# HGRN: odd heads mirrored instead of odd chunks, and POOL's low part in four pieces

## The chip, the cores and the metric

One core of one Trainium2 chip runs the whole program in one launch. The metric is the device time in microseconds (us), median of the runs shown. The engines are TensorE (PE), VectorE (DVE), ScalarE (ACT), GpSimd (POOL) and SyncE (SP); each works through its own queue, and they are tied by semaphores only.

## The reference

Two transformer blocks at sequence length 512 and width 1024, all in float32. The first has an HGRN2 mixer (8 heads of 128), an MLP of 4096 with squared ReLU, latent attention and a second MLP; the second has sparse attention, a state-space mixer and a gated feed-forward layer of 2816 with short convolutions. The change touches the HGRN2 mixer and the preparation of weights:

```python
q = silu(xn @ w_q); forget = lb + (1 - lb) * sigmoid(xn @ w_f); k = 1 - forget; v = xn @ w_i
# per head and chunk, b = cumsum(log(forget)) along time:
scores = einsum('bhtd,bhsd,bhtsd->bhts', q, k, exp(b_t - b_s) for s <= t else 0)
o = scores @ v + (q * exp(b)) @ state
state = exp(b_last) * state + (k * exp(b_last - b)).T @ v
out = (rmsnorm(o, g_norm) * silu(xn @ w_g)) @ w_o
```

## The kernel before

**Weights.** All large weights come as one stream of 375 tiles of 128x1024 in four slots. A float32 product is made of three fp32r products: x_hi with w_hi, x_lo with w_hi, x_hi with w_lo. SP loads the raw tile (L397), POOL issues a cast DMA for w_hi (`cast`, L404) and subtracts, w_lo = w_raw - w_hi, in one operation of 1024 columns (L431). POOL's queue is: subtraction of tile t, cast of tile t+3, subtraction of tile t+1. A cast waits for `slots_free`, which TensorE raises when the first product of a tile is done, so the subtraction of the next tile starts about when TensorE starts a tile; TensorE waits for `lo_ready` at each tile's start.

**HGRN stage.** `xh`, `xl` hold x times gain (features on partitions, 512 time steps on columns = 4 chunks of 128). TensorE runs 32 half units (4 pairs of heads p; for each, first the lower half of the contraction for four column blocks m = 0..3, then the upper half; m = 0, 1 are forget of the two heads, 2, 3 their queries; each half unit is half a tile), 16 steps for v (units 32 to 47, L817), and 8 gate units. The banks 0 to 3 hold the sums. VectorE scales them (`scaled`, hgrn_z), ACT takes the tanh, and VectorE makes forget, keys or queries (`finish`), after which `hm_free` lets TensorE use the bank again.

**Levels.** The scores in a chunk with their decays come from 8 steps (n = 0..7) for each pair: n = 0 is the diagonal, then block sizes L = 1, 2, .. 64. At each, TensorE multiplies the packed keys of left half blocks with the queries of right half blocks (`level`, L737: 4 products of 128 columns), VectorE multiplies keys and queries by the block decays (L2086, L2087), forms the next decays (L2088), drains, raises `lv_next`, and writes the scores by `copy_predicated` (L2093). ACT packs the keys (`pack`, L1432) after `lv_next`, and TensorE's next level waits for the packing. A packed array of 128 columns holds 64 keys of one chunk and 64 of another. So that these don't collide, the odd chunks of 128 time steps are mirrored in time throughout the stage (`straight`, `mirrored`, `plain`): x, the row of rstd, the keys, queries and v.

The order of levels among the units is written out in `LEVEL_UNITS`: level n of pair p stands at unit 8p + 10 + 2n, so from one pair to the next two levels can share a unit.

## Time and profile before

| | |
|---|---|
| median of 3 runs | 2534.12 us (2533.71 to 2537.46) |
| profiled execution | 2532.07 us, its span 2530.2 us |
| TensorE busy | 2452.8 us (97%), mean granted clock 0.994 |
| VectorE busy | 1536.5 us (61%) |
| POOL busy | 1135.1 us (45%) |
| ACT busy | 689.0 us (27%) |

The span is the time from the first to the last instruction; the time of the execution has 1.9 us around it. Busy shares are means over stages with different limits. A product of TensorE is pipelined, so its shown duration (0.39 us) is longer than the step from one to the next (0.23 us).

### The profile page before, as it was taken

What the parts mean: (1) busy time and instruction counts of PE and PEld (TensorE: products, weight loads), DVE (VectorE), ACT (ScalarE), POOL (GpSimd) and SP (SyncE); (2) the same over time, 40 slices, a digit from 0 to 9 for tenths busy, and PEclk for the clock granted to TensorE, in tenths of its full rate; (3) what the DMA queues carried; (4) which work ended last, traced back from release to release, by engine and by line L of the source; (5) the groups of instructions that cost most, each with busy time, mean ns of one, the idle gap of its engine ahead of it and who ended that gap; (6) DMA issues with size and microseconds to landing.
All of it is one profiled execution on the core that took longest, in us unless ns stands there. A gap on an engine that the chain in (4) does not pass through costs nothing.

```text
span 2530.2 us, 30245 instructions
## 1 busy us (share of the span) xinstructions
PE 2452.8 (97%) x11271; PEld 1967.8 (78%) x11271; DVE 1536.5 (61%) x2130; ACT 689.0 (27%) x1383; POOL 1135.1 (45%) x760
## 2 busy tenths in 40 slices
PE   8889999999989999999999999999999999999997
PEld 7778888888767778888888677777767777888886
DVE  6874665365655644654656794656655786777711
ACT  3113531021244431200212313333322542322201
POOL 4334455555532225555555344333333335555554
PEclk9999999999999999999999999999999999999999
DMA  6334456565642225556565465555555546655554
GB/s 208 117 117 149 151 190 198 187 197 190 200 142 81 91 88 196 191 191 199 184 216 183 134 211 183 175 167 175 166 179 179 189 135 204 194 190 198 187 196 166
DMA packets 147862, 436.28 MB, mean 172 GB/s; under 512 B 14560, under 2 KB 14736, under 8 KB 147728
## 3 DMA queue, kind: packets, MB, share of 16 engines
q1 hardware_dynamic: 64752, 200.29, 26.5%
q0 software_dynamic: 64176, 198.73, 22.2%
q10 hardware_dynamic: 18800, 35.47, 4.2%
q8 instruction: 84, 1.38, 0.2%
q14 instruction: 50, 0.41, 0.0%
HBM read 415.27 MB, written 16.80 MB: 171 GB/s over the span
## 4 chain that ended last, share of the span: by engine, by line
PE 41%; issue 29%; POOL 23%; DVE 5%; DVEq 1%; ACT 1%; DMA 0%; POOLq 0%; SPq 0%; ACTq 0%
POOL w_lo L431 19%; PE bank L488 11%; PE bank L491 11%; PE bank L490 11%; POOL w_hi L404 5%; PE bank L1205 1%; PE bank L1199 1%; DVE mla_probs L2565 1%; PE bank L737 1%; PE bank L1227 1%; DVEq L2089 1%; PE bank L817 1%; DVE hgrn_keys L2086 1%; PE bank L820 1%; PE bank L819 1%
## 5 line engine op out<-in xcount | busy, mean ns | idle before, releaser
L431 POOL TENSOR_TENSOR w_lo<-w_raw,w_hi 128x1024 fp32r<-128x1024 f32 x375 | 902.2, 2406 | 8.0
L404 POOL DMA_DIRECT2D w_hi<-stream x375 | 227.1, 606 | 1361.5 <-PE bank L488 1199.7
L488 PE MATMUL bank<-x_hi,w_hi 128*128 128x512 f32 x1464 | 586.6, 401 | 12.9 <-DVE x_lo L2005 5.3
L491 PE MATMUL bank<-x_hi,w_lo 128*128 128x512 f32 x1464 | 572.4, 391 | 0.0
L490 PE MATMUL bank<-x_lo,w_hi 128*128 128x512 f32 x1464 | 571.8, 391 | 0.0
L488 PEld LDWEIGHTS bank<-x_hi,w_hi 128*128 128x128 f32 x1464 | 276.0, 189 | 87.2 <-issue 18.1
L491 PEld LDWEIGHTS bank<-x_hi,w_lo 128*128 128x128 f32 x1464 | 275.8, 188 | 59.5
L490 PEld LDWEIGHTS bank<-x_lo,w_hi 128*128 128x128 f32 x1464 | 276.3, 189 | 56.3 <-issue 2.2
L2197 DVE TENSOR_TENSOR relu_sq<-relu 128x512 f32<-128x512 f32 x64 | 179.1, 2798 | 98.5 <-ACT relu L1530 98.5
L488 PE MATMUL bank<-hidden_hi,w_hi 128*128 128x512 f32 x512 | 199.2, 389 | 0.0
L490 PE MATMUL bank<-hidden_lo,w_hi 128*128 128x512 f32 x512 | 199.2, 389 | 0.0
L491 PE MATMUL bank<-hidden_hi,w_lo 128*128 128x512 f32 x512 | 199.2, 389 | 0.0
L1530 ACT ACTIVATE relu<-bank 128x512 f32<-128x512 f32 x64 | 38.3, 599 | 405.3 <-PE bank L491 405.3
L490 PEld LDWEIGHTS bank<-hidden_lo,w_hi 128*128 128x128 f32 x512 | 96.1, 188 | 20.0
L491 PEld LDWEIGHTS bank<-hidden_hi,w_lo 128*128 128x128 f32 x512 | 96.1, 188 | 19.9
L488 PEld LDWEIGHTS bank<-hidden_hi,w_hi 128*128 128x128 f32 x512 | 96.1, 188 | 19.9
L488 PE MATMUL bank<-x_mlp_hi,w_hi 128*128 128x512 f32 x256 | 100.1, 391 | 0.6 <-POOL w_lo L431 0.6
L491 PE MATMUL bank<-x_mlp_hi,w_lo 128*128 128x512 f32 x256 | 99.6, 389 | 0.0
L490 PE MATMUL bank<-x_mlp_lo,w_hi 128*128 128x512 f32 x256 | 99.6, 389 | 0.0
L2554 DVE TENSOR_TENSOR bank<-bank,toeplitz 128x128 f32<-128x128 f32 (+1 forms) x64 | 25.5, 398 | 114.7 <-PE bank L1199 112.8
L2208 DVE TENSOR_TENSOR mlp_scaled<-bank,mlp_rstd 128x512 f32<-128x512 f32 x16 | 11.1, 692 | 110.1 <-PE bank L491 110.1
L1760 ACT ACTIVATE mla_probs<-bank,mla_neg_max 128x128 f32<-128x128 f32 (+1 forms) x64 | 33.8, 529 | 149.9 <-DVE mla_neg_max L2556 148.6
(449 smaller groups left out, 4372.5 us busy)
## 6 DMA issues: line engine op xcount, KB each, us to landing
w_hi<-stream POOLq DMA_DIRECT2D x375, 512.0 KB, 4.7
w_raw<-stream SPq DMA_DIRECT2D x375, 512.0 KB, 3.7
projections<-spill_out ACTq DMA_DIRECT2D x56, 256.0 KB, 2.0
ssm_x<-projections ACTq DMA_DIRECT2D x4, 1024.0 KB, 8.0
gate_tiles<-projections ACTq DMA_DIRECT2D x16, 256.0 KB, 3.3
ssm_z<-projections ACTq DMA_DIRECT2D x16, 256.0 KB, 3.3
residual<-x_in SPq DMA_DIRECT2D x4, 512.0 KB, 6.6
toeplitz<-bias_by_distance POOLq DMA_DIRECT2D x4, 512.0 KB, 7.0
```

What stands on the lines that cost most here:

```text
L404: e.dma_start(in_slot(whi, t % SLOTS, o), in_stream(o)).then_inc(hi_ready[t % SLOTS], 16)
L431: e.tensor_tensor(wlo[:, s, :], raw[:, s, :], whi[:, s, :].bitcast(F32), ALU.subtract).then_inc(lo_ready, 1)
L488: mm = e.matmul(out, wh, rh, start=first, stop=False)
L490: e.matmul(out, wh, rl, start=False, stop=False)
L491: return e.matmul(out, wl, rh, start=False, stop=last)
L737: mm = e.matmul(o.rearrange("p (v n l) -> p v n l", v=2, l=L), left, right, start=True, stop=True)
L817: mm = e.matmul(o, xh[:, k, chunk(t)], wh, start=k == 0, stop=False)
L819: e.matmul(o, xl[:, k, chunk(t)], wh, start=False, stop=False)
L1530: e.activation(r_[:, j, :], bank[j][:, :], ACT.Relu).then_inc(f.free, 1)
L1760: e.activation(mpr[:, n % 3, 0:wd], bank[n % 3][:, 0:wd], ACT.Exp, scale=-1.0, bias=mnm[:, n:n + 1], accum_out=mrs[:, n:n + 1]).then_inc(a ...
L2197: tt(t_[:, j, :], r_[:, j, :], r_[:, j, :], ALU.mult)
L2554: tt(near, near, bias[:, ::-1], ALU.add)
```

## The change

1. All four chunks of the odd heads are mirrored in time, in place of the odd chunks of all heads. x and rstd stay in order; `scaled` writes hgrn_z of odd heads mirrored (reading PSUM backwards), the output of odd heads is read backwards (`head_order`), and v of the odd heads is flipped in each chunk by products with a flip matrix on TensorE in gate units 0 and 1, copied back by ACT.
2. A packed array holds 64 keys of an even head and 64 of an odd one. Keys and queries of a level are one operation of 512 columns each instead of two of 256; `lv_keys` is raised after the keys, and ACT packs on it; TensorE waits for both `lv_next` and `lv_packed`.
3. `hm_free` is gone: TensorE waits for `hm_z`.
4. Levels of odd pairs stand one unit earlier. The mask transposes stay after unit 4, the sum for rstd moves behind unit 5.
5. x_gained, the logarithm of rstd, hi and low are one operation instead of two.
6. POOL's subtraction is four operations of 256 columns, with one signal after the last.

```diff
         e.wait_ge(hi_ready[s], 16 * (t // SLOTS) + (16 if s else 0))
-        e.tensor_tensor(wlo[:, s, :], raw[:, s, :], whi[:, s, :].bitcast(F32),
-                        ALU.subtract).then_inc(lo_ready, 1)
+        for q in range(4):
+            cut = slice(256 * q, 256 * q + 256)
+            low = e.tensor_tensor(wlo[:, s, cut], raw[:, s, cut], whi[:, s, cut].bitcast(F32), ALU.subtract)
+        low.then_inc(lo_ready, 1)
...
 def mirrored(x):

+    return x.rearrange("p (c t) -> p c t", c=ST)[:, :, ::-1]
+
+def head_order(hh, x):
+
+    return mirrored(x) if hh % 2 else four(x)
+
+def half_blocks(x, p, L, right):
+
+    return bass.AP(tensor=x[:].tensor, offset=2 * p * S + (L if right else 0),
+                   ap=[[HEADS * S, P], [S - L if right else S + L, 2], [2 * L, S // (2 * L)], [1, L]])
+
+def block_decays(x, L, right):
+
+    n = S // L
+    return bass.AP(tensor=x.tensor, offset=x.offset + (1 if right else 0),
+                   ap=[list(x.ap[0]), [n - 1 if right else n + 1, 2], [2, n // 2], [0, L]])
...
-LEVEL_UNITS = [[(p, n) for p in range(4) for n in range(8) if 8 * p + 10 + 2 * n == u] for u in range(64)]
+LEVEL_UNITS = [[(p, n) for p in range(4) for n in range(8) if 8 * p + 10 - p % 2 + 2 * n == u] for u in range(64)]
...
 PACKED = [x for x in SLOT_ORDER if x[1] < 7]
-PACK_AT = {x: k for k, x in enumerate(PACKED)}
+KEYED = [x for x in SLOT_ORDER if x[1] >= 1]
+PACK_AT, KEY_AT = ({x: k for k, x in enumerate(xs)} for xs in (PACKED, KEYED))
...
             else:
+                e.wait_ge(lv_next, SLOT_AT[p, n - 1] + 1)
                 e.wait_ge(lv_packed, PACK_AT[p, n - 1] + 1)
+                if k0 >= 4:
+                    e.wait_ge(lv_used, k0 - 3)
+                L, b = LEVELS[n - 1], bank[4 + k0 % 4]
+                for c in range(ST):
+                    right = bass.AP(tensor=hqs[:].tensor, offset=2 * p * S + c * P + L,
+                                    ap=[[HEADS * S, P], [S - L, 2], [2 * L, 64 // L], [1, L]])
+                    mm = e.matmul(b[:, chunk(c)].rearrange("p (v n l) -> p v n l", v=2, l=L),
+                                  lkeys[PACK_AT[p, n - 1] % 2][:, c, :], right, start=True, stop=True)
+                mm.then_inc(lv_full, 1)
+                return
             for q in range(2):
...
+                hh, b = 2 * p + q, bank[4 + (k0 + q) % 4]
+                if k0 + q >= 4:
+                    e.wait_ge(lv_used, k0 + q - 3)
+                for c in range(ST):
+                    mm = e.matmul(b[:, chunk(c)], hks[:, hh, chunk(c)], hqs[:, hh, chunk(c)],
+                                  start=True, stop=True)
+                mm.then_inc(lv_full, 1)
...
             if kh == 0 and p:
-                e.wait_ge(hm_free, 4 * (p - 1) + m + 1)
+                e.wait_ge(hm_z, 4 * (p - 1) + m + 1)
...
             if u == 4:
+                e.wait_ge(consts_loaded, 16)
+                for n in range(7):
+                    mm = e.transpose(bank[4 + n // 4][:, chunk(n % 4)], col("levels", n * P, P), ident)
+                mm.then_inc(mk_full, 1)
+            if u == 5:
...
                 mm.then_inc(hr_col, 1)
-            if u == 4:
-                for n in range(7):
-                    mm = e.transpose(bank[4 + n // 4][:, chunk(n % 4)], col("levels", n * P, P), ident)
-                mm.then_inc(mk_full, 1)
...
                         if n == 0:
-                            e.wait_ge(hm_free, 12 + t + 1)
+                            e.wait_ge(hm_z, 12 + t + 1)
...
                 e.wait_ge(lv_used, 36)
+                e.wait_ge(hv_free_a, 4)
+                e.wait_ge(hv_free_d, 4)
+            if r < 2:
+                if r:
+                    e.wait_ge(kt_nat, 1)
+                for c in range(ST):
+                    o = bank[2 + c // 2][:, 256 * (c % 2):256 * (c % 2) + 256]
+                    odd = hv[:, c, 512 * r:512 * r + 512].rearrange("p (h v d) -> p h v d", v=2, d=P)[:, :, 1, :]
+                    e.matmul(o.rearrange("p (h d) -> p h d", d=P), col("flip", 0, P), odd, start=True, stop=True)
...
             e.wait_ge(kt_full, hh + 1)
+            if hh < 2:
+                for b in range(2):
+                    odd = hv[:, 2 * b:2 * b + 2, 512 * hh:512 * hh + 512]
+                    odd = odd.rearrange("p c (h v d) -> p c h v d", v=2, d=P)[:, :, :, 1, :]
+                    e.activation(odd, bank[2 + b][:, :].rearrange("p (c h d) -> p c h d", c=2, h=2), ACT.Copy)
...
                 e.wait_ge(oo_sum, hh)
-            e.activation(hos[:, :], bank[6][:, :], ACT.Square).then_inc(oo_sq, 1)
+            e.activation(four(hos[:, :]), head_order(hh, bank[6][:, :]), ACT.Square).then_inc(oo_sq, 1)
...
             e.wait_ge(oo_og, hh + 1)
-            e.activation(plain(ogh[:, hh, :], 0), straight(hgt[:, hh, :]), ACT.Copy)
-            e.activation(plain(ogh[:, hh, :], 1), mirrored(hgt[:, hh, :]), ACT.Copy).then_inc(oo_hi, 1)
+            e.activation(ogh[:, hh, :], hgt[:, hh, :], ACT.Copy).then_inc(oo_hi, 1)
...
                 e.wait_ge(lv_full, banks_before(SLOT_AT[p_, n_ + 1]) + 1)
-            e.wait_ge(lv_next, SLOT_AT[p, n] + 1)
+            if n == 0:
+                e.wait_ge(qk_ready, p + 1)
+            else:
+                e.wait_ge(lv_keys, KEY_AT[p, n] + 1)
             for v in range(2):
...
             e.wait_ge(hm_full, m + 1)
-            stt(hz[:, m % 2, :], bank[b][:, :], 0.5, hrs[:, :], ALU.mult, ALU.mult).then_inc(hm_z, 1)
+            hh = m % 2 if m < 16 else 0
+            stt(four(hz[:, m % 2, :]), head_order(hh, bank[b][:, :]), 0.5, head_order(hh, hrs[:, :]),
+                ALU.mult, ALU.mult).then_inc(hm_z, 1)
...
                 e.drain()
-                ts(hks[:, hh, :], f, -1.0, 1.0, ALU.mult, ALU.add).then_inc(hm_free, 1)
+                ts(hks[:, hh, :], f, -1.0, 1.0, ALU.mult, ALU.add)
             else:
-                mm = stt(hqs[:, hh, :], hsg[:, m % 2, :], 1.0, hz[:, m % 2, :], ALU.add, ALU.mult).then_inc(hm_free, 1)
+                stt(hqs[:, hh, :], hsg[:, m % 2, :], 1.0, hz[:, m % 2, :], ALU.add, ALU.mult)
...
             e.wait_ge(hm_sig, 16 + r + 1)
-            stt(hgt[:, r, :], hsg[:, r % 2, :], 1.0, hz[:, r % 2, :], ALU.add, ALU.mult).then_inc(hm_free, 1)
+            stt(hgt[:, r, :], hsg[:, r % 2, :], 1.0, hz[:, r % 2, :], ALU.add, ALU.mult)
...
             e.wait_ge(lv_full, k0 + 1)
+            k, q = half_blocks(hks, p, L, False), half_blocks(hqs, p, L, True)
...
             two = was.rearrange("p (n u) -> p n u", u=2)
-            for v in range(2):
-                k = half_blocks(hks, 2 * p * S, L, False, 4, v)
-                q = half_blocks(hqs, 2 * p * S, L, True, 4, v)
-                tt(k, k, block_decays(was, L, True, v), ALU.mult)
-                tt(q, q, block_decays(was, L, False, v), ALU.mult)
+            tt(k, k, block_decays(was, L, True), ALU.mult).then_inc(lv_keys, 1)
+            tt(q, q, block_decays(was, L, False), ALU.mult)
...
             e.drain().then_inc(lv_next, 1)
-            mask = lmask[(n - 1) // 4][:, (n - 1) % 4, :, :].bitcast(I32)
             for v in range(2):
-                src = bank[4 + k0 % 4][:, :].rearrange("p (c v n l) -> p c v n l", c=4, v=2, l=L)[:, :, v, :, :]
-                e.copy_predicated(half_blocks(hsc, 2 * p * S, L, True, 4, v),
-                                  mask[:, v, :].rearrange("p (n l) -> p n l", l=L).unsqueeze(1)
-                                  .broadcast_to([P, 4, 64 // L, L]), src)
+                mask = lmask[(n - 1) // 4][:, (n - 1) % 4, v, :].bitcast(I32)
+                o = hsc[:, 2 * p + v, :].rearrange("p (c n u l) -> p c n u l", c=ST, u=2, l=L)[:, :, :, 1 - v, :]
+                src = bank[4 + k0 % 4][:, :].rearrange("p (c v n l) -> p c v n l", c=ST, v=2, l=L)[:, :, v, :, :]
+                e.copy_predicated(o, mask.rearrange("p (n l) -> p n l", l=L).unsqueeze(1)
+                                  .broadcast_to([P, ST, 64 // L, L]), src)
```

## Rows read from the trace of the kernel before

**Rows 1.** The page, costliest groups: line, engine, operation, tiles, count | busy us, mean ns | idle.

```profile
L431 POOL TENSOR_TENSOR w_lo<-w_raw,w_hi 128x1024 fp32r<-128x1024 f32 x375 | 902.2, 2406 | 8.0
...
L2197 DVE TENSOR_TENSOR relu_sq<-relu 128x512 f32<-128x512 f32 x64 | 179.1, 2798 | 98.5 <-ACT relu L1530 98.5
```

**Rows 2.** Windows: stretch, length, busy us of each engine, clock share, DMA share, GB/s.

```profile
0.00:310.00 310.00, 285.61 (x1432) 238.54 (x1433) 205.22 (x389) 98.08 (x179) 120.78 (x84) 0.97 0.47 147
310.00:2530.00 2220.00, 2167.16 (x9840) 1729.29 (x9838) 1331.30 (x1742) 590.92 (x1205) 1014.34 (x677) 1.00 0.54 176
107.00:112.00 5.00, 5.00 (x19) 4.37 (x20) 4.52 (x11) 0.63 (x1) 0.00 (x0) 0.66 0.02 5
147.00:153.00 6.00, 5.49 (x24) 4.89 (x25) 2.17 (x6) 0.52 (x1) 0.00 (x0) 0.62 0.00 0
```

**Rows 3.** Waits of TensorE, 0 to 310 us: total us, times, longest us.

```profile
PE bank L737 <- ACT level_keys L1432: 7.1, 3, 2.6
PE bank L817 <- DVE hgrn_queries L2060: 6.8, 1, 6.8
PE bank L488 <- DVE x_lo L2005: 5.3, 2, 4.7
PE bank L817 <- ACT hgrn_v L1447: 2.2, 1, 2.2
...
PE bank L488 <- DVE hgrn_keys L2058: 1.2, 2, 0.8
```

**Rows 4.** Timeline of VectorE in HGRN: start us, us, what [idle before, releaser].

```profile
70.23 3.03 DVE L2088 TENSOR_TENSOR hgrn_decays<-hgrn_decays 128x256 f32<-128x256 f32 x1
...
127.55 0.69 DVE L2047 SCALAR_TENSOR_TENSOR hgrn_z<-bank,hgrn_rstd 128x512 f32<-128x512 f32 x1 [2.90 <-PE bank L491]
...
140.58 2.72 DVE L2086 TENSOR_TENSOR hgrn_keys<-hgrn_keys,hgrn_decays 128x256 f32<-128x256 f32 x1
...
146.17 0.69 DVE L2047 SCALAR_TENSOR_TENSOR hgrn_z<-bank,hgrn_rstd 128x512 f32<-128x512 f32 x1
```

**Rows 5.** Chain that ended last, 50 to 54 us: start us, us, what.

```profile
52.00 1.78 PE bank L727 x16
```

**Rows 6.** Timeline of POOL, first and last subtractions.

```profile
5.41 1.30 POOL L417 TENSOR_TENSOR w_lo<-w_raw,w_hi 128x512 fp32r<-128x512 f32 x1 [4.97 <-ACT w_hi L1478]
...
2505.68 7.10 POOL L431 TENSOR_TENSOR w_lo<-w_raw,w_hi 128x1024 fp32r<-128x1024 f32 x3
```

**Rows 7.** Timeline of an up stage, 352 to 358 us, POOL and VectorE.

```profile
352.20 0.57 POOL L404 DMA_DIRECT2D w_hi<-stream  x1 [2.44 <-PE bank L488]
...
352.42 3.34 DVE L2197 TENSOR_TENSOR relu_sq<-relu 128x512 f32<-128x512 f32 x1 [0.62 <-ACT relu L1530]
...
352.80 2.41 POOL L431 TENSOR_TENSOR w_lo<-w_raw,w_hi 128x1024 fp32r<-128x1024 f32 x1
...
355.95 0.69 DVE L2200 TENSOR_TENSOR hidden_lo<-relu_sq,hidden_hi 128x512 f32 x1 [0.19 <-issue]
...
357.64 0.57 POOL L404 DMA_DIRECT2D w_hi<-stream  x1 [2.44 <-PE bank L488]
```

**Rows 8.** Timeline of POOL, casts behind the first and last short tile.

```profile
559.35 0.57 POOL L404 DMA_DIRECT2D w_hi<-stream  x1 [0.87 <-PE bank L488]
...
2352.74 0.57 POOL L404 DMA_DIRECT2D w_hi<-stream  x1 [0.93 <-PE bank L488]
```

**Rows 9.** Waits of TensorE from 310 us on.

```profile
PE bank L994 <- ACT mla_probs L1622: 5.5, 4, 2.0
PE bank L1227 <- DVE mla_probs L2565: 5.2, 7, 0.8
...
PE bank L488 <- POOL w_lo L431: 3.7, 5, 1.0
...
PE bank L488 <- DVE x_lo L1959: 2.5, 2, 1.4
```

**Rows 10.** Line L2743: count, ns min/median/max, first and last start us.

```profile
L2743 DVE SCALAR_TENSOR_TENSOR ffn_gate<-ffn_tanh,ffn_gate x22: 680/2516/3187, 2175.8 to 2402.8; 128x512 f32<-128x512 f32 x22
```

More of the change, by code:

```diff
@@ L269, in build @@
         lbt = at("hgrn_lbt", 204.5, [P, 3, 8])
-        lkeys = [at(f"level_keys{x}", 176 + 2 * x, [P, 4, P]) for x in range(2)]
+        lkeys = [at(f"level_keys{x}", 176 + 2 * x, [P, ST, P]) for x in range(2)]
         lmask = [at(f"level_mask{x}", kb, [P, 4, 2, 64]) for x, kb in enumerate((8, 198))]
@@ L537, in build @@
         hr_sum, hr_row, hr_col, hr_done = sem("x_sum_full"), sem("x_rstd_ready"), sem("x_rstd_col_full"), sem("x_rstd_col")
-        hm_full, hm_free = sem("hgrn_m_full"), sem("hgrn_m_free")
+        hm_full = sem("hgrn_m_full")
         hm_z, hm_sig = sem("hgrn_z_ready"), sem("hgrn_sig_ready")
@@ L719, in level @@
                     else:
+                        e.wait_ge(lv_next, SLOT_AT[p, n - 1] + 1)
                         e.wait_ge(lv_packed, PACK_AT[p, n - 1] + 1)
-                    for q in range(2):
-                        hh, b = 2 * p + q, bank[4 + (k0 + (q if n == 0 else 0)) % 4]
-                        if k0 + q >= 4 and (n == 0 or q == 0):
-                            e.wait_ge(lv_used, k0 + (q if n == 0 else 0) - 3)
-                        if n == 0:
-                            for c in range(ST):
-                                mm = e.matmul(b[:, chunk(c)], hks[:, hh, chunk(c)], hqs[:, hh, chunk(c)],
-                                              start=True, stop=True)
-                        else:
-                            L = LEVELS[n - 1]
-                            for c in range(2):
-                                first = hh * S + 2 * P * c
-                                left = lkeys[PACK_AT[p, n - 1] % 2][:, 2 * q + c, :]
-                                right = bass.AP(tensor=hqs[:].tensor, offset=first + L,
-                                                ap=[[HEADS * S, P], [P - L, 2], [2 * L, 64 // L], [1, L]])
-                                o = b[:, 256 * q + P * c:256 * q + P * c + P]
-                                mm = e.matmul(o.rearrange("p (v n l) -> p v n l", v=2, l=L), left, right,
-                                              start=True, stop=True)
-                        if n == 0 or q == 1:
-                            mm.then_inc(lv_full, 1)
@@ L1492, in _ @@
             e.wait_ge(hr_sum, 1)
-            e.activation(plain(hrs[:, :], 0), straight(bank[7][:, :]), ACT.Ln, scale=1.0 / D, bias=col("eps"))
-            e.activation(plain(hrs[:, :], 1), mirrored(bank[7][:, :]), ACT.Ln, scale=1.0 / D, bias=col("eps"))
+            e.activation(hrs[:, :], bank[7][:, :], ACT.Ln, scale=1.0 / D, bias=col("eps"))
             e.drain()
@@ L2007, in x_gained @@
                 def x_gained(j):
-                    ts(plain(xnt[:, j % 4, :], 0), straight(h[:, j, :]), col("hgrn_norm", j), None, ALU.mult)
-                    ts(plain(xnt[:, j % 4, :], 1), mirrored(h[:, j, :]), col("hgrn_norm", j), None,
-                       ALU.mult).then_inc(xs_nt, 1)
+                    ts(xnt[:, j % 4, :], h[:, j, :], col("hgrn_norm", j), None, ALU.mult).then_inc(xs_nt, 1)
                 def x_add(a, b):
@@ L2111, in gated_out @@
                     e.wait_ge(oo_sq, hh + 1)
-                    stt(hgt[:, hh, :], bank[6][:, :], col("g_norm"), hgt[:, hh, :], ALU.mult, ALU.mult).then_inc(oo_raw, 1)
+                    stt(four(hgt[:, hh, :]), head_order(hh, bank[6][:, :]), col("g_norm"), four(hgt[:, hh, :]),
+                        ALU.mult, ALU.mult).then_inc(oo_raw, 1)
                 def normed_out(hh):
@@ L2119, in low @@
                     e.wait_ge(oo_hi, hh + 1)
-                    hi = ogh[:, hh, :].bitcast(F32)
-                    tt(plain(ogl[:, hh, :], 0), straight(hgt[:, hh, :]), plain(hi, 0), ALU.subtract)
-                    tt(plain(ogl[:, hh, :], 1), mirrored(hgt[:, hh, :]), plain(hi, 1), ALU.subtract).then_inc(oo_lo, 1)
+                    tt(ogl[:, hh, :], hgt[:, hh, :], ogh[:, hh, :].bitcast(F32), ALU.subtract).then_inc(oo_lo, 1)
                 for u in range(32):
```

21 lines of the change are left out of this document (4 added, 17 removed).

## The prediction

> **What bounds the kernel now.** I read the time by stage first. From 310 us on TensorE is busy 2167.16 of 2220 us; in the HGRN stage, the first 310 us, it is busy 285.61, so 24 us are idle there, and part of the rest runs at a clock share of 0.66 or 0.62 [rows 2]. The change lives almost wholly in these 310 us, except for one line, the subtraction of w_lo on POOL, which runs 375 times through the whole kernel [rows 1].
>
> Next, what TensorE waited for in the HGRN stage [rows 3]: 7.1 us in three waits for packed level keys, 6.8 us in one wait for hgrn_queries, 5.3 us at the start for x_lo, 2.2 us for hgrn_v, 1.2 us for hgrn_keys. All hang on VectorE (ACT packs what VectorE wrote). Then VectorE itself [rows 4]: the product at 70.23 us takes 3.03 us, and the one at 140.58 us takes 2.72 us for 256 columns. Both lie over a w_lo subtraction. The clearest case is in an up stage [rows 7]: relu_sq starts at 352.42, POOL's subtraction runs 352.80 to 355.21, and relu_sq ends at 355.76, 0.55 us after it; the same sort of operation next to it takes 0.69. So an operation of VectorE with two SBUF inputs stands still while POOL subtracts. Over 64 relu_sq this costs 179.1 - 64 x 0.69 = 135 us of VectorE, which is 51 blockings of 2.65 us [rows 1, 7], nearly all hidden there, because TensorE waits for POOL or VectorE in few places after 310 us [rows 9].
>
> **How late POOL may be.** In the ordinary pace a tile takes 357.64 - 352.20 = 5.44 us. Before the next cast POOL idles 2.44 us [rows 7]; the cast waits until TensorE has begun a tile. Some tiles hold less work, and there TensorE waits for w_lo (3.7 us in five waits [rows 9]) and POOL idles only 0.87 to 0.93 us before the cast, the way of the signal there and back. There are 8 such short tiles, the first and the last of them in [rows 8]. So an ordinary tile has 2.44 - 0.93 = 1.51 us to spare, a short one nothing.
>
> **The change, term by term** (minus is faster).
>
> *Price of a piece.* One 512-column subtraction takes 1.30 us [rows 6], one of 1024 takes 2.406 [rows 1]: 2.16 ns a column and 0.19 fixed. Three in a row take 7.10, so each is 0.04 shorter in a row [rows 6]. A piece of 256 is then 0.75, or 0.71 in a row, and four are 2.86: 0.46 us more for each tile. Bounds: 0, if the fixed part hides behind the piece in front, and 4 x 0.75 - 2.41 = 0.58. I take 0.46.
>
> *Does VectorE get in between two pieces?* No row shows two POOL subtractions in a row with VectorE waiting. For it: POOL gets in between VectorE operations that follow each other without a gap (relu_sq and the product at 70.23 both met a subtraction that started on time [rows 4, 7]), so the handing over works that way round. Against it: VectorE asks at 352.42, while POOL still issues its cast, and is not let in between the cast's end at 352.77 and the subtraction at 352.80 [rows 7]. I take it that it gets in. The Trainium skill says the same (SBUF — State Buffer, "Who interferes with whom"): whichever starts first has the shared port pair for the whole instruction, and the other blocks fully. By that rule a wait is one piece, 0.7 us, and not 2.65, which gives the sums below; the trace agrees that the blocking lasts the whole instruction (355.21 + 0.55).
>
> *HGRN, TensorE work.* Added: 8 fp32 products of 256 columns that flip hgrn_v of the odd heads. 8 of 128 columns take 1.78 us [rows 5], so 8 of 256 take +3.6 us. They stand in gate units 0 and 1, where TensorE sets the pace, so nothing hides them. Bound above +5, if the new waits in front of them (all 36 banks, hgrn_v free, kt_nat) are met late; below 3.6 nothing. The level products keep their number (4 of 128 columns).
>
> *HGRN, the level path.* Before, four products of 256, then the decays, then a drain released the packing; TensorE waited for the packing. Now key and query products are one of 512 each (0.69 for two of 0.42 that overlap to about the same), and the first alone releases ACT, so packing runs beside the query product and the decays. At 70.23 the blocked operation is just the last one, the decays. Odd pairs come one unit earlier, so a unit holds one level where it held two, and VectorE's idle time before the busy stretch (2.90 us before 127.55 [rows 4]) takes one level. At stake: 7.1 us of waits and the slow clock behind them, 5 x 0.34 = 1.7 us in 107 to 112 [rows 2], which I count once more for the third wait: 10.5. I take -8.0 (0 to -10.5).
>
> *HGRN, the bank waits.* hm_free becomes hm_z. The gain is smaller than it looks: hgrn_z of the last unit starts at 146.17 and the query products that released TensorE follow at once [rows 4], so the new semaphore alone is worth 0.6 us of the 6.8. The rest must come from one level (about 3 us) less in VectorE's queue ahead of it. With the slow clock behind, 6 x 0.38 = 2.3, at stake are 9.1; I take -6.0 (-1 to -9).
>
> *HGRN, start and rest.* x_gained as one operation and a shorter block at the second pair of x tiles: of 4.7 us I take -2.0 (0 to -4.7). The 1.2 us for hgrn_keys go, since hm_z comes before the keys: -1.2. x_sum one unit later delays ACT's logarithm and with it the first hgrn_z by half a tile, 5.44 / 2 = 2.7 us. Behind that wait in VectorE's queue stand the level masks and the first four hgrn_z; TensorE is then in units 6 and 7 and needs the first bank only in unit 8, so nothing (bound +2.7). No DMA is moved; SP's and POOL's queues keep their order, and POOL's cast stands behind four operations instead of one, which is the price of the pieces above. hgrn_v: the level of pair 3 now stands at the end of unit 39, and ACT must pack it before it empties the bank; the wait of 2.2 becomes about 2.9, +0.7. One operation for two in hi, low and the logarithm, and the mirrored reads of PSUM, lie off the path (no row shows such a read on VectorE; there are 12, 8 for hgrn_z and 4 for the gated output; at half as much again, 0.35 each, they add 4 us to the 205.22 that VectorE is busy of 310 [rows 2], so 0 to +2 on the path).
>
> HGRN together: 3.6 - 8.0 - 6.0 - 2.0 - 1.2 + 0.7 = -12.9.
>
> *After 310 us.* Gains: TensorE waits of 5.2 us for mla_probs, 2.5 for x_lo L1959 and 5.5 for ACT behind such an operation [rows 9]. I take 4.5 + 1.5 + 2.0 = -8.0 (0 to -11). Losses at 8 short tiles: 8 x 0.46 = 3.7, and port turns of VectorE of 0.55 inside them, of which I assume five, 2.8: +6.5 (3.7 with none, 9 with ten). Losses at ordinary tiles: two VectorE operations inside a subtraction make it 0.46 + 2 x 0.55 = 1.56 longer against 1.51 to spare. So 0.05 for 51 up tiles [rows 1] and 22 ffn tiles (L2743, median 2.5 us where 0.68 is undisturbed [rows 10]): 73 x 0.05 = +3.7 (0 to 24, the rival below). Together +2.2.
>
> Sum: -12.9 + 2.2 = -10.7. The profiled execution took 2532.07 us (span 2530.2), so 2521.4; the median of the runs is 2.05 higher, which I add: **2523 us**.
>
> **Rivals.**
> *POOL keeps the port through all four pieces.* Then a blocking is 0.46 longer, not shorter. The gains after 310 us go, the short tiles cost 3.7, the seven waits for mla_probs [rows 9] grow by 0.46 each, 3; HGRN keeps its order and signals, but the level path gives -5.5 and the start -0.5, so -8.9. Sum -2.2, 2532 us. For it is the missed turn at 352.77 [rows 7]. The Trainium skill has a rule for it (GPSIMD Engine Reference, 2.1 Instruction dispatch): the completion of a Pool instruction does not hold back the next one, each core starts on it when its own share is done. By that the port need never be free between pieces. That three in a row overlap by 0.04 us each agrees.
>
> *VectorE's turns make w_lo late (slower).* If each turn holds the port for all of 0.69 and no fixed part of a piece hides behind it, a tile is 0.46 + 1.38 - 1.51 = 0.33 late, 73 times: 24 in place of 3.7. Sum +9.7, 2544 us. It decides from 0.20 us a tile on (14.4 / 73), which is a turn of 0.62. Against it are the 0.55 after POOL's end [rows 7].
>
> *VectorE stays the bound in HGRN.* Its work per level hardly falls, and TensorE meets it at other places: levels -4, bank wait -2. Sum -2.7, 2531 us. Against it is the idle time it has before its busy stretches.
>
> **How the numbers follow.** Chances: forecast 0.46 (own range 2512 to 2529), POOL keeps the port 0.28 (2526 to 2538), VectorE's turns 0.18 (2538 to 2555), VectorE the bound 0.08 (2526 to 2536). 0.2%, 5 us, is about what a measurement of this kernel can tell from no change. Faster: 0.43 + 0.08 + 0.03 = 0.54. Same: 0.02 + 0.18 + 0.01 + 0.05 = 0.26. Slower: 0.01 + 0.02 + 0.17 = 0.20. The range leaves out one in ten on each side: 2511 to 2544.
>
> **What would show it.** Right: w_lo pieces of about 0.7 us, 2.9 a tile or 4.0 with two VectorE turns between them; relu_sq near 1.3 us in the mean and not 2.8; the waits of [rows 3] under 9 us in all; the mla_probs waits of [rows 9] gone; w_lo waits at short tiles about 1.3 us each. relu_sq at 3.3 or more shows that POOL keeps the port. Tiles over 5.44 us in the up and ffn stages, with TensorE waiting for w_lo, show the slower rival. HGRN waits for level_keys in new places show the last one. The prediction is wrong in its base if the mirrored reads slow VectorE.

## The result, and the profile after

The changed kernel took 2548.81 us (median of 4 runs, 2548.37 to 2554.44) against 2533.91 for the kernel before: ratio 1.0067, 95% interval 1.0053 to 1.0081. It is slower by 15 us by the medians and by 17 by the ratio; the forecast was 2523 us, its range ended at 2544. The profiled execution was the longest of the four, 2554.44 us (span 2552.6), 5.6 us over the median.

The page first: POOL's pieces and the same VectorE product as in [rows 1] (line, engine, operation | busy us, mean ns | idle).

```profile
L433 POOL TENSOR_TENSOR w_lo<-w_raw,w_hi 128x256 fp32r<-128x256 f32 x1500 | 1089.6, 757 | 10.2 <-DMA w_hi<-stream 2.0
...
L2207 DVE TENSOR_TENSOR relu_sq<-relu 128x512 f32<-128x512 f32 x64 | 199.9, 3123 | 83.3 <-ACT relu L1543 83.3
```

The windows, as in [rows 2]:

```profile
0.00:310.00 310.00, 288.27 (x1440) 239.44 (x1441) 200.97 (x314) 98.24 (x172) 146.74 (x194) 0.97 0.46 146
310.00:2530.00 2220.00, 2167.88 (x9811) 1728.09 (x9811) 1358.81 (x1734) 588.40 (x1202) 1168.54 (x1683) 1.00 0.54 175
```

The columns behind the length are TensorE's products and weight loads, VectorE, ScalarE and POOL. VectorE is busy 27.5 us longer than before from 310 us on, and 4.2 us less in the first 310.

TensorE's waits before 310 us (beside [rows 3]):

```profile
PE bank L814 <- DVE hgrn_z L2059: 5.2, 1, 5.2
PE bank L725 <- DVEq L2100: 4.7, 2, 2.7
PE bank L814 <- ACT hgrn_v L1461: 3.5, 1, 3.5
PE bank L490 <- POOL w_lo L433: 2.7, 2, 2.5
PE bank L490 <- DVE x_lo L2018: 2.1, 2, 1.4
PE bank L490 <- DVEq L2146: 1.9, 1, 1.9
```

And from 310 us on (beside [rows 9]):

```profile
PE bank L490 <- POOL w_lo L433: 10.2, 14, 1.3
PE bank L1233 <- DVE mla_probs L2575: 8.0, 7, 1.2
```

The timeline of an up stage, the place of [rows 7]:

```profile
355.43 0.57 POOL L404 DMA_DIRECT2D w_hi<-stream  x1 [2.03 <-PE bank L490]
355.65 3.76 DVE L2207 TENSOR_TENSOR relu_sq<-relu 128x512 f32<-128x512 f32 x1 [0.21 <-ACT relu L1543]
...
356.03 2.83 POOL L433 TENSOR_TENSOR w_lo<-w_raw,w_hi 128x256 fp32r<-128x256 f32 x4
```

Four pieces take 2.83 us, and relu_sq, asked for ahead of the row as in [rows 7], ends at 359.41, 0.55 us behind the last piece: it now stands still for all four. Its mean rose from 2798 to 3123 ns, where the forecast had 1.3 us. TensorE's waits for mla_probs rose from 5.2 to 8.0 us in the same seven places; those for w_lo rose from 3.7 to 10.2 us, and from five places to fourteen. In HGRN the waits for packed keys are gone, but waits for the drain behind the decays (L2100) and for hgrn_z stand in their place: those of [rows 3] make 22.6 us together, the six here 20.1.

A few tiles look otherwise. The timeline at the end of HGRN's output projection, VectorE, POOL and TensorE:

```profile
326.41 0.74 POOL L404 DMA_DIRECT2D w_hi<-stream  x1 [1.89 <-PE bank L490]
...
326.74 1.05 DVE L1974 SCALAR_TENSOR_TENSOR x_lo<-residual,consts,x_hi 128x512 fp32r<-128x512 f32 x1
...
327.17 4.64 POOL L433 TENSOR_TENSOR w_lo<-w_raw,w_hi 128x256 fp32r<-128x256 f32 x4
...
327.89 1.05 DVE L1985 TENSOR_TENSOR square_sum<-square_sum,next_squares 128x512 f32<-128x512 f32 x1
...
328.86 1.22 DVE L1974 SCALAR_TENSOR_TENSOR x_lo<-residual,consts,x_hi 128x512 fp32r<-128x512 f32 x1
...
330.19 1.04 DVE L1985 TENSOR_TENSOR square_sum<-square_sum,next_squares 128x512 f32<-128x512 f32 x1
...
331.95 0.47 PE L490 MATMUL bank<-x_hi,w_hi 128*128 128x512 f32 x1 [0.63 <-POOL w_lo L433]
```

Here VectorE does get in between pieces: none of its operations waits for more than one, the four pieces stretch to 4.64 us, and TensorE waits 0.63 us for w_lo. In 28 of the 375 tiles the four pieces take over 3.1 us, as here, 11 of them in the first 310 us. In 128 others a VectorE operation takes over 3 us across the row, and in the rest neither is seen. So both of the forecast's rivals for the pieces happened, the one in 128 tiles and the other in 28. The two kinds differ in the cast ahead of the row: it took 0.74 us or more in 23 of the 28, as at 326.41, and 0.57 in 122 of the 128, as at 355.43. Counted in the same way, split_only (below) has 23 of 26 and 123 of 126. Why a cast takes longer, and whether that lets VectorE in or only comes with it, no run shows.

### The profile page after: what moved, and what is told of

It reads as the page before. It is cut to its first block, busy times and chain, and to the rows that moved or that the text cites. A ratio compares the mean times of both kernels' runs of the same rounds, so it can differ in the third digit from the quotient of the medians.

```text
span 2552.6 us, 31328 instructions
## 1 busy us (share of the span) xinstructions
PE 2466.0 (97%) x11287; PEld 1974.4 (77%) x11287; DVE 1566.6 (61%) x2058; ACT 690.0 (27%) x1378; POOL 1321.7 (52%) x1885
## 4 chain that ended last, share of the span: by engine, by line
PE 33%; POOL 29%; issue 28%; DVE 7%; DVEq 1%; DMA 1%; ACT 1%; POOLq 0%; SPq 0%; ACTq 0%
POOL w_lo L433 24%; PE bank L490 9%; PE bank L493 9%; PE bank L492 9%; POOL w_hi L404 5%; PE bank L1211 1%; PE bank L1205 1%; DVE mla_probs L2575 1%; DVE dsa_work L2426 1%; DVE hgrn_decays L2099 1%; DVEq L2100 1%; PE bank L725 0%; DVE dsa_score L2533 0%; PE bank L1233 0%; PE bank L814 0%
## 5 line engine op out<-in xcount | busy, mean ns | idle before, releaser
L433 POOL TENSOR_TENSOR w_lo<-w_raw,w_hi 128x256 fp32r<-128x256 f32 x1500 | 1089.6, 757 | 10.2 <-DMA w_hi<-stream 2.0
L492 PE MATMUL bank<-x_lo,w_hi 128*128 128x512 f32 x1464 | 573.5, 392 | 0.0
L492 PEld LDWEIGHTS bank<-x_lo,w_hi 128*128 128x128 f32 x1464 | 277.1, 189 | 56.0 <-issue 2.4
L2207 DVE TENSOR_TENSOR relu_sq<-relu 128x512 f32<-128x512 f32 x64 | 199.9, 3123 | 83.3 <-ACT relu L1543 83.3
L492 PE MATMUL bank<-hidden_lo,w_hi 128*128 128x512 f32 x512 | 199.3, 389 | 0.0
L493 PEld LDWEIGHTS bank<-hidden_hi,w_lo 128*128 128x128 f32 x512 | 96.1, 188 | 20.1
L492 PEld LDWEIGHTS bank<-hidden_lo,w_hi 128*128 128x128 f32 x512 | 96.1, 188 | 19.7
L492 PE MATMUL bank<-x_mlp_lo,w_hi 128*128 128x512 f32 x256 | 99.7, 389 | 0.0
```

Source lines behind the costliest of these rows:

```text
L433: low = e.tensor_tensor(wlo[:, s, cut], raw[:, s, cut], whi[:, s, cut].bitcast(F32), ALU.subtract)
L492: e.matmul(out, wh, rl, start=False, stop=False)
L493: return e.matmul(out, wl, rh, start=False, stop=last)
L2207: tt(t_[:, j, :], r_[:, j, :], r_[:, j, :], ALU.mult)
```

## The experiments

Ratios are to the kernel before on the same chip, which took 2531.6 to 2532.2 us there. A difference between two of these ratios is uncertain by some 3 us.

**The two halves of the change apart.** hgrn_only has the one subtraction back, split_only is the kernel before with the four pieces.

```diff
-                for q in range(4):
-                    cut = slice(256 * q, 256 * q + 256)
-                    low = e.tensor_tensor(wlo[:, s, cut], raw[:, s, cut], whi[:, s, cut].bitcast(F32), ALU.subtract)
-                low.then_inc(lo_ready, 1)
+                e.tensor_tensor(wlo[:, s, :], raw[:, s, :], whi[:, s, :].bitcast(F32),
+                                ALU.subtract).then_inc(lo_ready, 1)
```

> The changed kernel with POOL's subtraction as one operation of 1024 columns again; all of the HGRN change stays. Theory K (the loss is the four pieces: longer work on POOL, a port kept longer, w_lo late): the loss goes, 2528 to 2534 us, near or a little under the kernel before, since behind the HGRN stage the changed kernel was only 1.4 us later, of which the pieces made a part. Theory H (the HGRN rearrangement makes the loss): 2545 us or more. If both have a share, between 2536 and 2544.

> The kernel before with POOL's subtraction in four pieces of 256 columns, HGRN untouched. Theory K: 2546 to 2554 us, slower by 13 to 20 us, w_lo waits of TensorE at 12 us or more in some 15 places, relu_sq at about 3.1 us in the mean. Theory H: within 5 us of the kernel before.

Measured: hgrn_only 2533.98 us, 1.0007 (0.9998 to 1.0016); split_only 2547.02 us, 1.0059 (1.0047 to 1.0071). The excesses add up to that of the whole, 1.0067. So the pieces cost some 15 us, and HGRN gains nothing.

**Dose and turns.** two_pieces is the changed kernel with two operations of 512 columns (the first edit below). drained has four pieces and a drain, which waits until what POOL has begun is done, behind each of the first three (the second edit).

```diff
-                for q in range(4):
-                    cut = slice(256 * q, 256 * q + 256)
+                for q in range(2):
+                    cut = slice(512 * q, 512 * q + 512)
...
+                    if q < 3:
+                        e.drain()
```

> The changed kernel with two pieces of 512 columns. If the price is the fixed part of each piece, 2 x 1.26 = 2.52 us a tile, so 0.12 over one operation against 0.43 for four: a loss of a quarter to a third of that of four pieces, 2531 to 2537 us. If the price is VectorE getting in between two pieces, at most one turn a tile is possible: 2530 to 2540 us and the sum of TensorE's w_lo waits near 5 us instead of 12.9.

> The changed kernel with a drain of POOL between two pieces, so that POOL's next piece isn't issued until the one before has ended. If VectorE is shut out because the next piece already stands in line for the port, it now gets in: relu_sq falls from 3.7 us in the median to about 1.3, and POOL's pieces stretch, 3 to 4.5 us a tile; the total is then open, 2545 to 2570 us, because every turn of VectorE makes w_lo later. If POOL keeps the port whatever stands in line, relu_sq stays above 3.7 us, and the total grows only by the drains: 2552 to 2560 us.

Measured: two_pieces 2538.41 us, 1.0025 (1.0016 to 1.0035), a piece 1299 ns, relu_sq 2858 ns, w_lo waits 7.3 us. The first of the two expected ranges ended at 2537 us and the second at 2540, so this run doesn't tell them apart; between hgrn_only at 1.0007 and the changed kernel at 1.0067 the loss goes about with the length of POOL's row. drained 3374.26 us, 1.3331 (1.3312 to 1.3350), where at most 2570 us was expected. Its timeline, POOL and VectorE:

```profile
460.98 0.74 POOL L433 TENSOR_TENSOR w_lo<-w_raw,w_hi 128x256 fp32r<-128x256 f32 x1
465.04 2.72 POOL L433 TENSOR_TENSOR w_lo<-w_raw,w_hi 128x256 fp32r<-128x256 f32 x3 [3.31 <-issue]
...
466.08 1.10 DVE L2209 TENSOR_TENSOR relu_sq<-relu 128x512 f32<-128x512 f32 x1 [4.98 <-ACT relu L1545]
```

relu_sq, which starts inside the row, takes 1.10 us and no more: it ends at 467.18, 0.56 us behind the second piece (465.90 to 466.62), and doesn't wait for the one after. None of the 64 takes over 1.67 us, and their mean is 874 ns. So with a drain behind each piece VectorE gets its turn. But the first drain behind a cast takes 3.31 us, TensorE waits 295 times for w_lo at L492, and the time goes up by a third.

**The late tiles.** split_spared is split_only with one operation in the 15 tiles for whose w_lo TensorE waited.

```diff
-                for q in range(4):
-                    cut = slice(256 * q, 256 * q + 256)
+                for q in range(1 if t in SPARED else 4):
+                    cut = slice(0, 1024) if t in SPARED else slice(256 * q, 256 * q + 256)
```

> The kernel before with its subtraction in four pieces, except in the 15 tiles of 375 in which the four pieces were waited for: there one operation of 1,024 columns stands again. Theory A: the loss of the four pieces has two parts, w_lo that comes late (11.1 us of TensorE's waits against 3.7 before), and VectorE operations that wait some 0.5 us longer for POOL everywhere else (mla_probs, x_lo and others). Sparing these 15 tiles takes away about half of the 15 us: ratio about 1.003, w_lo waits back to 3 to 5 us in all. Rival: the whole loss comes from the tiles in which VectorE gets between the pieces, and the other waits follow from them: ratio 1.000 to 1.001. Second rival: the wait only moves on to the next tile that is as short of time, and the ratio stays at 1.005 to 1.006.

Measured: 1.0029 (1.0018 to 1.0040). TensorE's waits from 310 us on, of split_only:

```profile
PE bank L490 <- POOL w_lo L433: 11.1, 15, 1.4
PE bank L1229 <- DVE mla_probs L2567: 8.0, 7, 1.2
```

And of split_spared:

```profile
PE bank L1231 <- DVE mla_probs L2569: 8.0, 7, 1.2
...
PE bank L492 <- POOL w_lo L435: 3.7, 5, 1.0
```

About half of the loss went with the 15 tiles, as the first theory had it, and the w_lo waits are those of [rows 9] again; the other half stayed, with mla_probs at 8.0 us.

**What lets VectorE in.** tail_ops is the kernel before with two operations of 5 columns behind the subtraction; tail_untold raises the signal behind them instead of ahead; pieces_told is split_only with a signal, waited for by nobody, behind each of the first three pieces.

```diff
                 e.tensor_tensor(wlo[:, s, :], raw[:, s, :], whi[:, s, :].bitcast(F32),
                                 ALU.subtract).then_inc(lo_ready, 1)
+                for q in range(2):
+                    e.tensor_tensor(tail[:, 1 + q, :], tail[:, 0, :], tail[:, 0, :], ALU.subtract)
+                e.drain()
...
-                low.then_inc(lo_ready, 1)
+                    low.then_inc(lo_ready if q == 3 else hi_begun, 1)
```

> The kernel before with its one subtraction of 1,024 columns a tile, w_lo told as ready after it as before, and behind it two POOL operations of 5 columns into a tile that nobody reads, with a drain behind them ahead of the next cast. w_lo is not later, only POOL's row of operations is some 0.3 to 0.4 us longer, as with four pieces. Theory: what is left of the loss when w_lo is on time (split_spared, 1.003) comes from POOL's row of operations, which VectorE waits for to the end as if it were one: relu_sq's mean rises from 2.79 to about 3.1 us, mla_probs waits from 5.2 to 7 or 8 us, ratio 1.002 to 1.003. Rival: operations on so few columns let VectorE in, relu_sq stays at 2.8 us and the ratio at 1.000 to 1.001; the loss then comes from the pieces as such.

> split_only, in which each of the first three pieces of a tile also raises a semaphore that nobody waits for. Theory A: POOL keeps the port from one operation to the next when nothing has to be told in between; with a semaphore after each piece VectorE gets in between pieces, relu_sq's mean falls from 3.13 to 1 to 2 us, more tiles stretch to over 3.3 us for their four pieces, and w_lo waits grow beyond 11 us: ratio 1.008 to 1.02. Theory B: the semaphore has no part in it, and the operation of 5 columns let VectorE in by its size: all as in split_only, relu_sq at 3.1 us, ratio 1.005 to 1.007.

> tail_ops with the semaphore for w_lo raised by the last of the two operations of 5 columns, not by the subtraction itself: three operations in a row with nothing told in between, and w_lo ready some 0.6 us later. Theory A (what is told matters): VectorE now waits to the end of the row, relu_sq's mean rises from 2.6 to 3.0 to 3.4 us, mla_probs waits to 7 or 8 us, ratio 1.003 to 1.007. Theory B (the size matters): relu_sq stays at 2.6 to 2.8 us; only the w_lo waits grow, by 0.6 us at each of some 8 short tiles: ratio 1.001 to 1.003.

Measured: tail_ops 1.0007 (0.9997 to 1.0018), relu_sq 2586 ns, mla_probs waits 5.5 us. A single wait of 4.6 us for w_lo at 27.82 us, where the added drain held POOL for 7.4 us behind the first casts, is in this; beyond it the row costs nothing that can be measured. relu_sq's mean is lower than before because some of the holds moved to hidden_lo: the two together are busy 238.3 us, 238.9 in the kernel before, and 257.7 in split_only. In its timeline of VectorE and POOL an operation met the subtraction and not the tail:

```profile
353.06 2.99 DVE L2206 TENSOR_TENSOR hidden_lo<-relu_sq,hidden_hi 128x512 f32 x1 [0.19 <-issue]
353.08 2.41 POOL L434 TENSOR_TENSOR w_lo<-w_raw,w_hi 128x1024 fp32r<-128x1024 f32 x1
355.44 0.81 POOL L437 TENSOR_TENSOR tail<-tail 128x5 f32<-128x5 f32 x2
```

It ends at 356.05, 0.56 us behind the subtraction and before the tail's end at 356.25. tail_untold 1.0022 (1.0013 to 1.0032) with relu_sq at 2708 ns and 240.0 us for the two: nearly the same, plus w_lo ready later, 5.8 us of waits from 310 us on. pieces_told 1.0058 (1.0045 to 1.0071), relu_sq 3131 ns: as split_only. So the signal has no part in it. Behind a subtraction, operations of 5 columns on a tile of their own let VectorE in, pieces of 256 mostly don't; where between them it turns, and whether by size or by operands, stays open.

**The terms of HGRN.** Three kernels from hgrn_only: no_flip leaves out the flip matmuls and ScalarE's copies (so the odd heads' v is unflipped and their output another), levels_unshifted puts the levels of odd pairs back, v_first evicts v ahead of the level of units 39 and 47.

```diff
-LEVEL_UNITS = [[(p, n) for p in range(4) for n in range(8) if 8 * p + 10 - p % 2 + 2 * n == u] for u in range(64)]
+LEVEL_UNITS = [[(p, n) for p in range(4) for n in range(8) if 8 * p + 10 + 2 * n == u] for u in range(64)]
...
-                    for k in range(8):
+                    for k in range(7):
                         for x in LEVEL_UNITS[32 + 8 * n + k]:
                             level(*x)
                     for t in (1, 3):
...
+                    for x in LEVEL_UNITS[39 + 8 * n]:
+                        level(*x)
```

> hgrn_only without the eight matmuls with the flip matrix and the four ScalarE copies back: the values of the odd heads stay in unflipped order, so this kernel leaves out the flip of v and the output of the odd heads is another. Theory: the flips stand on TensorE's path with their own 1.8 us per half, 3.6 us in all, and nothing hides them: 2530.4 us where hgrn_only has 2534, ratio to the kernel before 0.9990 to 0.9995. Rival: most of it is behind the keys and updates that TensorE would wait for anyway: a gain of at most 1.5 us, ratio 1.000 to 1.0005.

> hgrn_only with one edit undone: the levels of the odd pairs of heads stand one unit later again, in the units where the kernel before has them. Theory: what took back the gain of the mirrored heads in HGRN is the place of the levels. One unit earlier, in an odd unit, VectorE's operations of a level fall into POOL's subtraction of each tile (small decays of 2.4 us, hgrn_keys of 3.2 us), TensorE waits 5.7 us at unit 32 and 4.0 us for hgrn_v at unit 40. With the levels back: these waits fall by 5 to 9 us, ratio to the kernel before 0.997 to 0.999. Rival: VectorE's order is as full either way and the waits only change their places: ratio 1.000 to 1.001, like hgrn_only.

> hgrn_only with the evictions of v ahead of the level of units 39 and 47, on VectorE and on ScalarE (the order that the kernel before has there). Theory: the wait of 4.0 us for hgrn_v at unit 40 is made by ScalarE's pack and VectorE's level of unit 39 that stand ahead of the evictions; with it gone the time falls by 3 to 4 us, ratio to the kernel before 0.9985 to 0.9997. Rival: the level of unit 41 then waits for its keys, packed after the evictions, and TensorE loses at L723 what it gained at L812: ratio as hgrn_only, 1.000 to 1.001.

Measured: no_flip 0.9992 (0.9983 to 1.0000), so the flips cost 3.8 us, give or take 3. levels_unshifted 1.0003 (0.9995 to 1.0012): the waits for hgrn_v fell from 4.7 to 1.8 us, but those at L723 rose from 4.6 to 7.8; my theory fell, the rival stands. v_first 0.9999 (0.9990 to 1.0007), between the two expectations: hgrn_v fell from 4.0 to 1.7, L723 rose to 5.9, so more than half of the wait only moved.

**HGRN without POOL's hold.** before_free and hgrn_free subtract 16 columns in tiles 4 to 31 and take w_hi for w_lo there, in the kernel before and in hgrn_only.

```diff
-                e.tensor_tensor(wlo[:, s, :], raw[:, s, :], whi[:, s, :].bitcast(F32),
+                cut = slice(0, 16 if 4 <= t < 32 else 1024)
+                e.tensor_tensor(wlo[:, s, cut], raw[:, s, cut], whi[:, s, cut].bitcast(F32),
                                 ALU.subtract).then_inc(lo_ready, 1)
```

> The kernel before with POOL's subtraction cut to 16 columns in tiles 4 to 31, the weights that HGRN reads up to its gates, and with w_hi taken in place of w_lo in their matmuls: it leaves out the low part of these weights and does as many matmuls. It is the base for hgrn_free. Theory: without POOL's holds of 2.4 us VectorE keeps up, and TensorE's waits before 310 us (22.9 us before) fall to 10 to 16 us: ratio 0.995 to 0.997. Rival: VectorE is late from its own work, the waits stay above 20 us: ratio 0.999 to 1.001.

> The same cut (POOL's subtraction to 16 columns in tiles 4 to 31, w_hi in place of w_lo there) in hgrn_only; it leaves out the same low part. Theory: the mirrored heads do take some 8 us of work off VectorE, but POOL's holds gave the time back; without them the kernel is 3 to 8 us faster than before_free, after the 3.6 us for the flips: ratio 0.992 to 0.995. Rival: the moved levels and the early keys change nothing that TensorE waits for, with or without POOL: 0 to 4 us slower than before_free, by the flips.

Measured: before_free 2519.11 us, 0.9952 (0.9938 to 0.9965); hgrn_free 2512.78 us, 0.9927 (0.9915 to 0.9939). TensorE's longest waits before 310 us in before_free:

```profile
PE bank L490 <- DVE x_lo L2007: 4.2, 3, 1.9
PE bank L819 <- DVE hgrn_queries L2062: 4.2, 1, 4.2
PE bank L819 <- ACT hgrn_v L1449: 2.2, 1, 2.2
```

And in hgrn_free:

```profile
PE bank L814 <- ACT hgrn_v L1461: 2.3, 1, 2.3
PE bank L490 <- DVE x_lo L2018: 1.7, 2, 1.4
```

With POOL out of the way the mirrored heads are 6.3 us faster, flips included, and not one wait for a level or for hgrn_z is left. With POOL in the way they are 1.8 us slower. The small product of the decays is one place where this is seen. VectorE's groups before 310 us, in the kernel before:

```profile
L2088 DVE TENSOR_TENSOR hgrn_decays<-hgrn_decays 128x256 f32<-128x256 f32 (+4 forms) x20 | 7.7, 383 | 0.0
```

In hgrn_only:

```profile
L2097 DVE TENSOR_TENSOR hgrn_decays<-hgrn_decays 128x256 f32<-128x256 f32 (+4 forms) x20 | 14.5, 723 | 0.0
```

And in hgrn_free:

```profile
L2099 DVE TENSOR_TENSOR hgrn_decays<-hgrn_decays 128x256 f32<-128x256 f32 (+4 forms) x20 | 5.2, 261 | 0.0
```

In before_free its mean is 255 ns. So POOL's holds cost this product 2.6 us in the kernel before and 9.3 with the mirrored heads.

**Out of POOL's way.** decays_last is v_first with the decays behind the masked copies; before_decays makes that one edit in the kernel before; z_early is decays_last with hgrn_z of unit 31 ahead of the level of unit 30.

```diff
-                    tt(decays_of(p, n - 1), two[:, :, 0], two[:, :, 1], ALU.mult)
                     e.drain().then_inc(lv_next, 1)
...
+                    tt(decays_of(p, n - 1), two[:, :, 0], two[:, :, 1], ALU.mult)
                     e.drain().then_inc(lv_used, 1)
...
-                        scaled(j, m)
+                        if u < 31:
+                            scaled(j, m)
                         if m:
                             finish(j - 1)
+                        if u == 30:
+                            scaled(15, 3)
```

> v_first, and in each level VectorE's product of the decays behind the masked copies, in place of ahead of the drain that lets TensorE start the next level. Theory: in v_first TensorE waits 5.9 us in HGRN for that drain, because the decays, an operation of 8 to 64 columns, are held up for up to 2.4 us by POOL's subtraction; off that path the waits at L723 fall to 1 to 3 us and the time by 3 to 5 us: ratio to the kernel before 0.998 to 0.9995, the first version under both kernels. Rival: the hold is met by the next operation in its place (the copies, then hgrn_z at unit 32), and TensorE waits as much elsewhere: ratio 0.9995 to 1.0005.

> The kernel before with the one edit of decays_last: the product of the decays behind the masked copies of a level. Theory: in the kernel before TensorE's waits for the levels end in ScalarE's pack after the drain, which the decays hold up too, so 2 to 5 us are to be had there as well: ratio 0.998 to 0.9995, about as decays_last. Rival: in the kernel before the hold of VectorE is met elsewhere in the level (twelve operations of 256 columns for eight), the ratio is 1.000, and the gain of decays_last needs the mirrored heads.

> decays_last, and VectorE's hgrn_z of unit 31 ahead of the level of unit 30 instead of behind it. Theory: TensorE's wait of 5.6 us at unit 32 is for this hgrn_z, queued behind a level that POOL's subtraction holds up; ahead of the level it is done as soon as unit 31's matmuls are: the wait falls to 0 to 2 us, and some of it comes back at the next levels: 2 to 6 us, ratio to the kernel before 0.996 to 0.9975. Rival: VectorE is late in all, the level of unit 30 then ends later by as much and TensorE waits there: ratio 0.998 as decays_last.

Measured: decays_last 0.9982 (0.9973 to 0.9992), before_decays 1.0009 (1.0001 to 1.0018), z_early 2521.98 us, 0.9955 (0.9943 to 0.9967), a little more than its theory expected. z_early beats both kernels, the one before by 10 us by the medians and 11 by the ratio. Its waits in HGRN:

```profile
PE bank L723 <- DVEq L2095: 3.7, 2, 3.2
PE bank L812 <- DVE hgrn_z L2055: 2.5, 1, 2.5
PE bank L488 <- DVEq L2145: 1.5, 1, 1.5
```

The edit of the decays gives nothing in the kernel before, where it costs 2 us if anything, against my theory. On top of the mirrored heads it gives 4.3 us (0.9999 to 0.9982, give or take 3). decays_last also lost its wait for hgrn_v; at L723 it still waits 4.4 us, where 1 to 3 were expected.

## Why the prediction was wrong

The forecast was 26 us too low. Two steps of it failed, and each is worth about half of that: the pieces (+2.2 forecast, +15 measured) and HGRN (-12.9 forecast, +1.8 measured).

**The first step that failed: "I take it that it gets in."** On this stood the gains of 8.0 us after 310 us, relu_sq near 1.3 us and, by the forecast's own rival, 2.5 us of the levels' gain and 1.5 of the start's. Where they meet, VectorE mostly waits for the whole row, and each hold is 0.42 us longer. The missed turn at 352.77 in [rows 7] was the row to trust, and it is no single case. In the trace before, 118 VectorE operations of 512 columns with both inputs in SBUF begin after a cast has begun and before the subtraction behind it: 113 of them are held and end 0.56 us behind the subtraction, whether they began 0.03 or 0.6 us ahead of it. The 61 that began in the 0.65 us ahead of a cast all ended in under 0.76 us. So the hold reached from the cast over the gap to the subtraction's end. The counter-argument was taken from the other direction, POOL getting in between VectorE's operations, and that says nothing about POOL's own row. The Trainium skill's rule (SBUF — State Buffer, "Who interferes with whom") that whoever issues first holds the pair for the whole instruction agrees with drained, 1.10 us for one piece. In [rows 7] it agrees only if POOL's cast counts as its start, since relu_sq began 0.38 us ahead of the subtraction. With 256 columns in a row the runs show the hold going over four instructions, 3.76 us, where the forecast drew from that rule a wait of one piece. What the Trainium skill says (GPSIMD Engine Reference, 2.1 Instruction dispatch), that a Pool instruction's completion does not hold back the next, fits this; no run shows the inside of it.

**Price of a piece.** Right: 2.83 us a tile, 0.42 more than one operation, forecast 0.46 (0 to 0.58).

**Short tiles.** At the 8 short tiles w_lo waits grew in split_only from 3.7 to 7.1 us, by 3.4, forecast 3.7. What was not in the sum are 7 late tiles that aren't short, 3.9 us in split_only: tiles whose row VectorE's turns had stretched. The forecast had 0.05 us a tile for this with two turns of 0.55; the tile shown has its four pieces 2.23 us longer than one operation, against 1.51 to spare. This is the rival "VectorE's turns make w_lo late", in a few tiles instead of 73.

**Where 15 us went.** split_only against before: w_lo +7.4, mla_probs +2.8, all listed waits from 310 us on 41.1 to 52.3, +11.2. In split_spared 6 us by the medians and 8 by the ratio go with the late tiles, while the waits for mla_probs stay. Of the other half the waits show 5.1 us (41.1 to 46.2); the last 3 to 4 us are not traced.

**The second step that failed: HGRN, -12.9 forecast, +1.8 measured** (hgrn_only, -0.5 to +4.1). Term by term:
- Flips +3.6: right, 3.8 by no_flip.
- Level path -8.0: waits fell only from 7.1 to 4.6. The forecast let the packing run beside the decays, and so it does; but TensorE waits for `lv_next` too, whose drain stands behind the decays, and these now meet POOL's subtraction more often (383 to 723 ns).
- Bank wait -6.0: 6.8 became 5.7. The level that was to leave the queue is gone, but hgrn_keys (L2069 in hgrn_only) is held 3.22 us, where it takes 0.43 in hgrn_free, just ahead of the level and of hgrn_z (the rows are below the list).
- Start -2.0: x_lo 5.3 became 3.6, about right (v_first and z_early, with the same start, have 1.4 and 1.2, so a single trace can't tell it better). x_sum one unit later was put at nothing, bound +2.7: there is a new wait of 1.5 us at unit 9, for the drain at L2144. hgrn_free has the same x_sum and not this wait, so it needs POOL's hold: hgrn_keys at 40.79 us, in the queue ahead of it, takes 2.62 us.
- hgrn_keys -1.2: right. hgrn_v +0.7: it became +1.8, and 0.7 more ahead of the flips.
- Mirrored reads of PSUM: no cost, hgrn_z 688 ns against 687.

```profile
134.95 0.74 POOL L404 DMA_DIRECT2D w_hi<-stream  x1 [4.14 <-PE bank L812]
135.15 3.22 DVE L2069 TENSOR_SCALAR hgrn_keys<-hgrn_forget 128x512 f32<-128x512 f32 x1
...
135.71 2.36 POOL L431 TENSOR_TENSOR w_lo<-w_raw,w_hi 128x1024 fp32r<-128x1024 f32 x1
```

So the wrong step here is that less work in VectorE's queue was counted as time. VectorE did 73 operations fewer and was busy longer, 215.4 for 205.2 us in the first 310 (hgrn_only), as its operations stood still for POOL. hgrn_free shows that the order of the work is good for -6.3, or -10.1 without the flips; z_early gets it back by taking two operations out of POOL's way. The third rival, "VectorE stays the bound in HGRN", described this stage and had a chance of 0.08. Its HGRN terms make -4.9, against +1.8 measured: the right kind, and too small. In the changed kernel itself VectorE is busy only 201.0 us in this stretch, 215.4 in hgrn_only, yet TensorE's waits there make 21.6 us in both.

**The rival "POOL keeps the port"** had the mechanism and the wrong size: 2532 us, with 8.9 us of gains in HGRN that didn't come and 6.7 us for the pieces where they cost 15. That two rivals could be right in one kernel, most tiles by the one and a few by the other, was in none of the cases, nor was an HGRN stage without any gain; the range ended 5 us short.

## What to carry to other kernels

Cutting an operation on POOL into pieces that follow each other at once made most waits of VectorE longer here, by the pieces' fixed cost. In the 28 tiles where VectorE did get in, its waits were shorter and POOL's row longer, and where TensorE needed w_lo at once, that lost time. Before counting work saved on an engine as time, look at what its operations meet when they move: the same saving was worth 6.3 us without POOL's holds and nothing with them. When a small operation stands ahead of a signal, ask whether it needs to: moving the decays behind it gave 4.3 us with the mirrored heads and nothing without.

## What the runs showed of the hardware

- VectorE waits through a row of four POOL subtractions of 256 columns (3.76 us), but not through two of 5 columns behind one of 1,024 (tail_ops); a signal between pieces changes nothing (pieces_told, relu_sq 3131 ns for 3133).
- A VectorE operation with two SBUF inputs that begins while POOL issues its cast is held till the subtraction behind the cast has ended (113 of 118 in the kernel before).
- Once VectorE is in between the pieces, they take turns: 4.64 us for four, VectorE's operations 1.04 to 1.22 us each. This went with casts of 0.74 us ahead of the row (23 of 28 tiles).
- An operation with a single SBUF input, hgrn_keys from hgrn_forget, is held as well: 3.22 us for 0.43.
- A drain on POOL behind a cast took 3.31 us (drained), and 7.4 us at the start, with three casts ahead of it (tail_ops).
- A POOL operation of 5 columns takes 313 ns in the mean (tail_ops), where the columns beyond the first 512 of a subtraction cost 2.16 ns each: nearly all of it is the operation's own price.
